# A hybrid encoder layer on one core: in the second part of the output projection, VectorE adds the residual of the next tile before it normalises this one

## What is computed

```python
def rmsnorm(x, gain):
    xf = x.astype(jnp.float32)
    y = xf * lax.rsqrt(jnp.mean(xf * xf, axis=-1, keepdims=True) + EPS)
    return (y * gain.astype(jnp.float32)).astype(x.dtype)
...
    mix = jnp.concatenate([multiscale_pool(u_pool, pool_w, pool_scale),
                           hgrn2_mixer(u_q, u_ff, u_fb, u_i, u_g, lb_fwd, lb_bwd, hg_norm_gain)], axis=-1)
    x = x + jnp.einsum('bse,ed->bsd', mix, w_out)
    x = x + hierarchical_moe(rmsnorm(x, norm_ffn), router_group_w, router_group_b,
                             router_expert_w, router_expert_b, w1, w3, w2)
```

## Time and profile before

| | us |
|---|---|
| median of 3 runs | 1730.1 |
| lowest and highest | 1728.18, 1734.45 |
| the profiled execution, its own time | 1726.82 |
| its span in the trace | 1725.2 |
| TensorE busy in the span | 1606.1 |
| VectorE busy | 533.2 |
| ScalarE busy | 400.5 |
| GpSimd busy | 165.0 |

### The profile page before, as it was taken

The page is one execution under the profiler, slowest core; times in us unless marked ns, Lnnn a source line. Parts: engine busy times, 40 slices in busy tenths (PEclk is TensorE's granted clock), DMA queues, the critical chain, the costliest instruction groups (busy, mean ns, idle before and its releaser), DMA issues.

```text
span 1725.2 us, 20747 instructions
## 1 busy us (share of the span) xinstructions
PE 1606.1 (93%) x7622; PEld 805.5 (47%) x7622; DVE 533.2 (31%) x1103; ACT 400.5 (23%) x604; POOL 165.0 (10%) x213
## 2 busy tenths in 40 slices
PE   6999999999989998999957999999999999999990
PEld 4444445545545554554434444444444444444440
DVE  5541034535525444543564111111111111111114
ACT  6011034455345343222420000000000000000004
POOL 2001000000000000001002011111111111111100
PEclk9999999999999999999977999999999999999995
DMA  7222142233131315344838899999999999999958
GB/s 238 85 94 79 61 134 68 68 102 107 51 116 68 128 56 182 113 153 153 310 142 313 298 339 337 333 334 335 333 333 334 335 332 336 333 335 335 333 174 304
DMA packets 171232, 371.59 MB, mean 215 GB/s; under 512 B 8992, under 2 KB 46368, under 8 KB 171040
## 3 DMA queue, kind: packets, MB, share of 16 engines
q1 hardware_dynamic: 152160, 304.62, 50.4%
q0 software_dynamic: 18720, 65.02, 12.4%
q10 hardware_dynamic: 288, 1.05, 0.1%
HBM read 304.60 MB, written 66.06 MB: 215 GB/s over the span
## 4 chain that ended last, share of the span: by engine, by line
PE 90%; DVE 3%; ACT 2%; issue 2%; DMA 2%; DVEq 0%; SPq 0%; ACTq 0%; POOLq 0%
PE bank L1423 29%; PE bank L1677 27%; PE bank L1701 14%; PE bank L1546 7%; PE bank L1670 2%; PE bank L1588 2%; PE bank L1505 2%; PE bank L1522 1%; PE bank L1521 1%; PE bank L1500 1%; PE bank L1692 1%; PE bank L1606 1%; PE bank L1453 1%; PE bank L1417 1%; ACT junk L946 1%
## 5 line engine op out<-in xcount | busy, mean ns | idle before, releaser
L1423 PE MATMUL bank<-wide,mid 128*128 128x512 f32 x1152 | 500.7, 594 | 3.9 <-issue 3.1
L1677 PE MATMUL bank<-wup,xgT 128*128 128x512 f32 x1088 | 480.2, 594 | 1.4 <-ACT xgT L926 1.4
L1423 PEld LDWEIGHTS bank<-wide,mid 128*128 128x128 f32 x1152 | 218.2, 191 | 273.9 <-issue 272.6
L1677 PEld LDWEIGHTS bank<-wup,xgT 128*128 128x128 f32 x1088 | 204.5, 191 | 246.2 <-issue 244.1
L1701 PE MATMUL bank<-wide,hidT 128*128 128x512 f32 x544 | 240.9, 596 | 4.2 <-DVE hidT L1384 4.2
L1701 PEld LDWEIGHTS bank<-wide,hidT 128*128 128x128 f32 x544 | 101.3, 191 | 119.4 <-issue 119.4
L1546 PE MATMUL bank<-early,mid 128*128 128x512 f32 x288 | 124.8, 592 | 0.0
L933 ACT ACTIVATE sil<-bank 128x512 f32<-128x512 f32 x34 | 20.3, 597 | 434.5 <-PE bank L1677 434.5
L1357 DVE TENSOR_SCALAR mid<-bank,gate_of 128x512 f32<-128x512 f32 x68 | 51.1, 751 | 212.2 <-PE bank L1701 212.2
L723 POOL DMA_INDIRECT x_dram<-mid,sidx x34 | 53.6, 1578 | 644.0 <-DVE mid L1357 297.3
L926 ACT ACTIVATE xgT<-bank 128x512 f32<-128x512 f32 x70 | 38.1, 594 | 273.1 <-PE bank L1670 273.1
(11 more groups left out here) (196 smaller groups left out, 1299.7 us busy)
## 6 DMA issues: line engine op xcount, KB each, us to landing
wup<-w SPq DMA_DIRECT2D x68, 2048.0 KB, 16.6
wide<-w SPq DMA_DIRECT2D x34, 2048.0 KB, 10.4
u_dram<-ustage POOLq DMA_DIRECT2D x60, 256.0 KB, 2.3
rin<-u_dram SPq DMA_DIRECT2D x60, 256.0 KB, 4.4
mid<-w_in SPq DMA_DIRECT2D x24, 512.0 KB, 4.0
early<-x_all SPq DMA_DIRECT2D x12, 512.0 KB, 3.8
mix_dram<-mixst POOLq DMA_DIRECT2D x24, 256.0 KB, 2.7
mid<-x_all SPq DMA_DIRECT2D x12, 512.0 KB, 5.4
```

The costliest lines, as they stand in the source:

```text
L1423: last = pe.matmul(PROJ[u % 3][:, :], wsec[:, slot, k, :], nT[:, k, g * GT:(g + 1) * GT], start=(k == 0), stop=(k == KT - 1))
L1677: last = pe.matmul(bank[out_bank][:, :], xgT[:, k, :], weights[:, s, k, :], start=(k == 0), stop=(k == KT - 1))
```

## The change

`residual(t)` keeps only the two additions. The wait for ScalarE's root, the reciprocal and the normalisation become `norm(t)`, and VectorE's order becomes residual(0), residual(1), norm(0), and then for t = 2 to 11: residual(t), norm(t-1), add_bias(t-2); at the end norm(11) and the last two add_bias. Since two tiles' sums of squares are now alive together, they get a slot each: `tile_ss` (16 bytes a partition) takes the place of `ss` in this stage, and the reciprocal goes to `rstd[:, s]`. The programs of TensorE, GpSimd and SyncE are unchanged, and ScalarE's changes only in the address of its sums.

```diff
         ss = sb(always, "ss", [P, 2])
+        tile_ss = sb(always, "tile_ss", [P, 2, 2])
         rstd = sb(always, "rstd", [P, 2])
...
-            def square_sum(done, count, x, junk, signal):
+            def square_sum(done, count, x, junk, s, signal):
 
                 act.wait_ge(done, count)
-                chain.link(act.activation(junk, x, ACT.Square, accum_out=ss[:, 0:1]))
-                act.activation(ss[:, 1:2], ss[:, 0:1], ACT.Sqrt, bias=eps_col[:, 0:1],
+                chain.link(act.activation(junk, x, ACT.Square, accum_out=tile_ss[:, s, 0:1]))
+                act.activation(tile_ss[:, s, 1:2], tile_ss[:, s, 0:1], ACT.Sqrt, bias=eps_col[:, 0:1],
                                scale=1.0 / D).then_inc(signal, 1)
...
                     dve.tensor_tensor(x1t[:, s, cs], bank[2 * s + half][:, :], xres[:, s, cs],
                                       ALU.add).then_inc(x1_ready, 1)
+
+            def norm(t, s):
+
                 dve.wait_ge(rms2_ready, t + 1)
-                link(dve.reciprocal(rstd[:, 0:1], ss[:, 1:2]))
-                dve.scalar_tensor_tensor(out=xnt[:, s, :], in0=x1t[:, s, :], scalar=rstd[:, 0:1],
+                link(dve.reciprocal(rstd[:, s:s + 1], tile_ss[:, s, 1:2]))
+                dve.scalar_tensor_tensor(out=xnt[:, s, :], in0=x1t[:, s, :], scalar=rstd[:, s:s + 1],
                                          in1=rowc[:, R_FFN:R_FFN + D], op0=ALU.mult,
                                          op1=ALU.mult).then_inc(xn_ready, 1)
...
             residual(0, 0)
             residual(1, 1)
+            norm(0, 0)
             chain.start()
             with dve.Fori(1, NT // 2) as i:
                 chain.enter(i - 1, 2)
                 for s in range(2):
                     residual(2 * i + s, s)
+                    norm(2 * i + (s - 1), 1 - s)
                     add_bias(2 * i + (s - 2))
             chain.leave(NT // 2 - 1)
+            norm(NT - 1, 1)
             add_bias(NT - 2)
             add_bias(NT - 1)
```

More of the change, by code:

```diff
@@ L899, in project @@
                     act.wait_ge(xnT_ready, 2 * t - 2)
-                square_sum(x1_ready, 2 * t + 2, x1t[:, s, :], xnt[:, s, :], rms2_ready)
+                square_sum(x1_ready, 2 * t + 2, x1t[:, s, :], xnt[:, s, :], s, rms2_ready)
             project(0, 0)
```

## The result

| | before | after | the change run again |
|---|---|---|---|
| median, us | 1730.12 | 1736.84 | 1738.72 |
| lowest and highest | 1728.18, 1734.45 | 1733.58, 1741.92 | 1736.06, 1739.09 |
| executions | 8 | 8 | 5 |
| ratio to the kernel before, 95% interval | | 1.0039 [1.0025, 1.0053] | 1.0049 [1.0035, 1.0062] |
| profiled execution, its span | 1726.82, 1725.2 | 1735.79, 1734.1 | 1736.08, 1734.3 |

The change makes the kernel slower by 6.7 us, 0.39%. The change was run again beside 21 executions of the kernel before (median 1730.08), and lost 8.6 us.

What follows compares the result with a forecast made beforehand. TensorE was taken to bound the stage at 5.415 us a tile; a new pace of 5.87 gives +2.8 us, less 0.2 for a sooner load: +2.6, median 1730.1 to 1732.7 us. Range: 1728.5 to 1739.5 us.

Steps and rivals of the forecast that it cites:

- the load's circle: Norm, two stores, `mixt` load, projection, addition, next norm: 11.74 us for two tiles, 5.87 a tile, taken as the pace.
- The store's landing: Time from issue to landing of the `x1t` store: taken as 2.7 us, against a median of 3.5 before.
- the store's circle: Norm, store issue, landing, addition two tiles on, next norm: 5.69 us a tile against 5.415 before.
- Start: First tiles of the stage: addition of tile 2 goes sooner, at 827.5; norm of tile 2 ends at 836.3.
- 8p - 44.2: Shift of the last addition's end for pace p over eight tiles from norm 2 to norm 10: +2.8 us at 5.87.
- The 0.2 us for the sooner load: At tile 3, a load no longer behind norm work starts the projection some 0.2 us sooner, subtracted from the shift.
- The clock: Rival: TensorE idles about 0.6 us a tile and its clock falls throughout; +25 us, 1755 us; chance 0.02.
- The tail: After the last addition, the router product of tile 10 starts as before: taken as 0, -0.9 us kept for the range.
- the margin of 0.6 us at the transposes: Norm of tile 4 ends at 847.97, TensorE's transposes of it start at 848.60: thin but enough.
- Hidden: Rival: store and load stay hidden, TensorE keeps 5.415 us a tile; shift -1.1 us, 1729.0 us; chance 0.12.
- Late stores: Rival: `x1t` stores land late behind the burst's last load; at 5.3 us, +22 us, 1752 us; chance 0.10.
- Addresses: The 16 bytes more of `tile_ss` move every later buffer: taken as 0; an effect either way had chance 0.02.

Runs made afterwards that it cites:

- with the load's circle opened: The changed kernel with four slots of `mixt`, loaded four tiles ahead, TensorE's and SyncE's loops written out: 1736.45 us, ratio 1.004 to the kernel before.
- with the store's opened: The changed kernel with four slots of `x1t`, each addition waiting for the store four tiles back, loops written out: 1735.40 us, ratio 1.0023 to before.
- with both open: The changed kernel with four slots of `mixt` and four slots of `x1t` together: 1728.45 us, ratio 0.9987 to the kernel before.
- the best version: The changed kernel with loads queued first, early `x1t` stores, squares' junk output in free space and four `mixt` slots: 1726.93 us, 0.998 to before.
- the same queue order: Loads of t+2, `x1t` store of t, `xnt` store of t-1; squares' junk apart: 1728.56 us with VectorE's new order, 1736.69 with its old.
- loads in front: The changed kernel with SyncE issuing the loads of tile t+3 ahead of the stores of tile t: 1752.71 us, ratio 1.0121 to before.
- only the addresses: The kernel after with the new slots of `tile_ss` but VectorE's old order: 1730.75 us against 1731.88, ratio 0.9991 to before.

## Why the prediction was right and where its size failed

*What bounds, and how.* Right. The prediction said that the norm moved behind the next addition closes two circles through the DMA queue of nearly the same length, 5.69 and 5.87 us a tile, and that the slower one takes over from TensorE's 5.415. The pace measured from norm 4 to norm 10 is 5.893 and 5.923. The runs show both: with the load's circle opened the store's holds 5.767 (5.69 by the prediction), with the store's opened the load's holds 5.797 (5.87), and with both open TensorE is the bound again.

*The store's landing.* The choice of 2.7 us, "because in the new order the last load was issued over three microseconds before each store", was right: 2.7 at the median. The Trainium skill (DMA: Bandwidth & Descriptors, section Anatomy of one DMA) fits a DMA of the GpSimd path with 2.0 us plus the bytes at 436 GB/s, an estimate of 3.2 us for this store, and the store's circle would have been 6.19. This store goes through SyncE's queue and the measurement decides.

*Start.* Right: norm 2 ends 21.76 us after the stage's first matmul (840.41 - 818.65), predicted 836.3 - 814.78 = 21.5.

*The step that failed* is the shift, "8p - 44.2": one pace p for all tiles from norm 2 on, with `mixt` read 4.76 us after the store's issue everywhere. From tile 7 on that figure holds (five bursts, the load down 4.7 to 5.1 us after the store's issue, mean 4.80). But in the burst issued at 840.60 it was down after 6.2 us (842.12 + 4.7 - 840.60), and TensorE started at 846.92; in the next burst it took 5.6. From norm 2 to norm 4 after took 14.89 us and the repeat 13.18, where the prediction had 11.74. Here is that burst as a whole, the queues and the DMA issues of after from 840 to 846 (count, size, us to landing):

```profile
q8 instruction: 1, 0.02, 1.0%
q14 instruction: 1, 0.01, 0.3%
...
x_dram<-wide SPq DMA_DIRECT2D x1, 512.0 KB, 3.3
xn_dram<-wide SPq DMA_DIRECT2D x1, 512.0 KB, 5.4
wide<-part_dram SPq DMA_DIRECT2D x1, 512.0 KB, 5.3
mid<-mix_dram SPq DMA_DIRECT2D x1, 128.0 KB, 4.7
```

And the issues of a usual one, the same view from 861 to 867:

```profile
x_dram<-wide SPq DMA_DIRECT2D x1, 512.0 KB, 2.7
xn_dram<-wide SPq DMA_DIRECT2D x1, 512.0 KB, 3.9
wide<-part_dram SPq DMA_DIRECT2D x1, 512.0 KB, 4.4
mid<-mix_dram SPq DMA_DIRECT2D x1, 128.0 KB, 3.6
```

Every DMA of the burst lands later, the second store by 1.5 us. In the kernel before, landings are spread anyway, its slowest store of `x1t` is that of the same tile 2 (issued at 833.36, landed after 5.7 us), and nothing waited for them that closely. Two packets of the queues that carry instructions fall into this window and none into the usual one. That is a coincidence in time, and neither kind is enough or needed by itself: a packet of q8 also falls between 834 and 840, where the stores land after 3.1 and 4.1 us, and with four slots of `x1t` the late burst has one of q8 and none of q14. No run here took them away, so the cause of the late burst stays open. It comes at the same tile in the repeat and with four slots of `x1t` (`xnt` stored in 5.4 and 5.5 us, `mixt` in 4.7 and 5.3).

In sums, from the stage's start to the end of its last addition: 64.21 us before. After: 64.21 + 2.8 as predicted + 0.24 (norm 2) + 3.15 (norms 2 to 4) + 0.14 (six tiles at 5.893 instead of 5.87) + 0.11 (last addition to norm 10 in 1.39 instead of 1.50) = 70.65, measured 70.62. In the repeat the same terms are 2.8 + 0.35 + 1.44 + 0.32 + 0.1 = 5.0, measured 69.19 - 64.21 = 4.98. (The 0.2 us for the sooner load is left out of the 2.8; it did not show.) So one pair of tiles makes 3.15 of the 3.8 us that were missed in the one profile, and 1.44 of 2.4 in the other. The time lies in the range, but its upper part was kept for a landing of 3.5 us or a late load at every tile, and neither came; that it also had room for one late burst and a fall of the clock is in part luck.

*The clock.* The rival had it fall throughout at 0.02, and it did not: the steady stretch is at 1.00 (2.4 GHz). It fell once, behind the 2.32 us of idling at the late burst: the windows go 0.88, 0.50, 0.77 (0.50 is the 1.2 GHz level), and the projection took 3.22 instead of 1.98, the transposes 1.52 instead of 1.04, 1.7 us in all, the main difference between the two 2-to-4 sums, 14.89 - 13.18. The repeat idled for 1.82 us there and kept its clock. So 1.7 of the 3.15 us is the clock at this one place, which the prediction had in no term of its sum.

*The tail.* Taken as 0 with -0.9 kept in the range (the two differences that the prediction names, 1.71 - 1.04 and 1.19 - 0.77, add up to 1.09). Measured from the last addition to the routing: 6.90 after against 7.92. But with the old order and the new slots it is 6.89. The tail is near 6.9 to 7.1 or 7.9 to 8.4 by whether the clock fell: it fell in 3 of the 4 profiles with the old order and in 2 of the 10 with the new. The new order may spare it more often, since its waits there come as 1.62 and 0.74 us instead of 2.14 in one piece, but four profiles against ten do not show it, and it is not the -1.0 us that the two first profiles alone would suggest.

*What would show it.* Waits for the store in most tiles, TensorE waiting for `mixt`: as written. Stores in 2.7 to 3 us: nine of twelve; the second and third took 3.1 and 3.3, the last 4.0. The wait of the reciprocal was to stay at the last tile and stayed at the first, 0.7 us. Pairs of 11.4 to 11.8 us: 11.86. Stage 75 to 76: 77.5 and 76.1 us. TensorE waits for the norm once, at the end; with the store's circle alone (four slots of `mixt`) it does so six times, four of them between the first transposes and the last two tiles, so the margin of 0.6 us at the transposes was as thin as the prediction said.

*The rivals.* Hidden: no, by the waits and the pace of both profiles of the change. Late stores: not in this kernel, but near its price when loads were put in front of them. Addresses: excluded by the run with the slots alone. The DMA engines' throughput, a rival that the prediction did not name: excluded by the best version, with a share of 0.94 at 5.208 us a tile.

*What stays open.* The stage accounts for +5.4 and +4.0 us, the medians say +6.7 [+4.3, +9.2] and +8.6 [+6.1, +10.7]. The repeat's profiled execution, 1736.08, is the second fastest of its five and 2.6 us below their median, so the unprofiled ones may have had more falls of the clock; no profile shows it. And there is one profile of the kernel before, of an execution 3.3 us below its median.

## What to carry to other kernels

Before moving a step behind another on an in-order engine, follow each buffer that the moved step frees round its whole circle (step, store issue, landing, next writer, back to the step) and each load that stands behind it in the queue: the slowest circle, not the wait removed, sets the new pace. An order of compute and an order of a queue belong together: the same queue order took the loss away from the new order (0.9996) and made the old one slower (1.0036). And where a circle has no slack, take its length from the worst burst as well as from the usual one, since each late transfer is then paid in full.

## What the runs showed of the hardware

- On SyncE's queue the DMAs of this stage landed in the order in which they were issued, in all fourteen profiles. A store of 512 KB with next to nothing ahead of it in the queue lands in 2.7 us, the next one, issued some 0.5 us behind it, 3.8 to 3.9 us after its own issue; behind loads of 640 KB the same store takes 4.7 to 5.6 (loads in front), and behind three DMAs up to 7.2 (`x1t` stored after its addition).
- So issuing a DMA earlier can make later ones land later: with the store of `x1t` moved ahead the median landing of `mixt` was 5.0 us (issued from 835 to 885) instead of 3.4 (from 842 on).
- The clock is not decided by the length of one idle stretch alone: it fell after 1.92 us of idling (four slots of `x1t`, at 847.80: projection 2.60, transposes 1.91 us) and after 2.32 (after, at 846.92), and held after 2.17 (only the addresses, at 885.04: transposes 1.09) and after 3.04 (loads in front, at 906.47: transposes 1.09, projection 1.88).
